# Eight conditioning slices in seven places, ahead of the second half of w_in

## What is computed

```python
cs = silu(c)                                  # 9 conditioning rows of 1024
mod = cs @ w_ada + b_ada                      # w_ada is 1024 x 6144, in float32 24 MB
sh1, sc1, g1, sh2, sc2, g2 = split(mod, 6)
h = rmsnorm(x, norm1_g) * (1 + sc1) + sh1
proj = h @ w_in                               # then two mixers (gated linear attention, windowed attention)
bias = rel_bias[rel_bucket(distance)]         # a table by distance, used by the attention later
```

## Time and profile before

| | |
|---|---|
| median of 3 runs | 1361.9 us (1361.71 to 1362.45) |
| the profiled execution | 1366.18 us, of which the span from first to last instruction is 1364.6 |
| busy, share of the span | TensorE 83%, DVE 51%, ACT 45%, POOL 9% |
| mean granted TensorE clock | 0.918 of full speed |
| moved by DMA | 234.43 MB, mean 172 GB/s |

### The profile page before, as it was taken

One profiled execution on the slowest core, in us unless ns is written; L12 is line 12 of the kernel. 1 busy time (PEld: TensorE's weight loads), 2 busy tenths in 40 slices (PEclk: granted clock), 3 DMA queues, 4 the chain that ended last, 5 costly groups with the idle time before them and its releaser, 6 DMA issues.

```text
span 1364.6 us, 18815 instructions
## 1 busy us (share of the span) xinstructions
PE 1126.3 (83%) x6935; PEld 630.3 (46%) x6936; DVE 702.5 (51%) x1099; ACT 607.8 (45%) x939; POOL 118.8 (9%) x135
## 2 busy tenths in 40 slices
PE   3799999898989898996799980089999999999800
PEld 0255656465656566664445540034444444444400
DVE  2356545454444444346333336257558658655557
ACT  2256553444454545345311121157557557555434
POOL 0000000000000000000100003320112111111032
PEclk9799988899999999998889995589999999999955
DMA  9664410605050413822325310569868798768255
GB/s 356 245 215 149 129 49 10 185 1 155 1 147 10 119 37 96 306 94 64 99 73 170 131 66 7 202 215 381 327 246 307 271 344 322 267 247 332 108 200 188
DMA packets 122341, 234.43 MB, mean 172 GB/s; under 512 B 11079, under 2 KB 54569, under 8 KB 119200
## 3 DMA queue, kind: packets, MB, share of 16 engines
q1 hardware_dynamic: 111760, 200.37, 43.1%
q0 software_dynamic: 7200, 21.06, 4.3%
q10 hardware_dynamic: 3312, 12.06, 2.2%
HBM read 197.60 MB, written 35.64 MB: 171 GB/s over the span
## 4 chain that ended last, share of the span: by engine, by line
PE 65%; DVE 12%; DMA 10%; issue 5%; ACT 5%; POOL 2%; SPq 0%; POOLq 0%; ACTq 0%; DVEq 0%
PE banks L1605 7%; PE banks L1606 7%; PE banks L1607 7%; PE banks L1971 4%; PE banks L1972 4%; PE banks L1973 4%; DMA arena<-in_moe_w_gate_dram 3%; PE banks L1793 3%; PE banks L1821 3%; PE banks L1807 3%; DVE arena L1496 2%; DVE arena L1264 2%; PE banks L1912 2%; DMA arena<-in_w_ada_dram 2%; PE banks L1913 2%
## 5 line engine op out<-in xcount | busy, mean ns | idle before, releaser
L1496 DVE SCALAR_TENSOR_TENSOR arena<-arena 128x2048 f16<-128x2048 f32 x96 | 217.5, 2288 | 82.7 <-ACT arena L972 82.7
L972 ACT ACTIVATE arena<-arena 128x2048 f16<-128x2048 f32 x96 | 180.2, 1906 | 94.2 <-DMA arena<-in_moe_w_up_dram 57.9
L1605 PE MATMUL banks<-arena 128*128 128x384 f16 (+5 forms) x576 | 193.4, 336 | 11.9 <-DVE arena L1158 8.2
L1606 PE MATMUL banks<-arena 128*128 128x384 f16 (+5 forms) x576 | 192.8, 335 | 0.0
L1607 PE MATMUL banks<-arena 128*128 128x384 f16 (+5 forms) x576 | 192.5, 334 | 0.0
L1971 PE MATMUL banks<-arena 128*128 128x512 f16 x368 | 141.5, 385 | 10.5 <-DVE arena L1509 10.4
L1972 PE MATMUL banks<-arena 128*128 128x512 f16 x368 | 141.2, 384 | 0.0
L1973 PE MATMUL banks<-arena 128*128 128x512 f16 x368 | 141.0, 383 | 0.0
L867 ACT ACTIVATE arena<-banks 128x512 f32<-128x512 f32 (+3 forms) x96 | 49.3, 513 | 128.7 <-PE banks L1807 128.7
L1264 DVE CUSTOM_DVE_ANT_0 arena<-banks,arena 128x128 f32<-128x128 f32 (+7 forms) x96 | 72.3, 754 | 45.9 <-PE banks L1793 45.7
L859 ACT ACTIVATE arena<-arena 128x128 f32<-128x128 f32 (+7 forms) x96 | 74.3, 774 | 28.8 <-DVE arena L1267 27.5
(11 more groups left out here) (308 smaller groups left out, 1704.3 us busy)
## 6 DMA issues: line engine op xcount, KB each, us to landing
arena<-in_moe_w_gate_dram SPq DMA_DIRECT2D x32, 1024.0 KB, 8.4
arena<-in_moe_w_up_dram SPq DMA_DIRECT2D x32, 1024.0 KB, 8.3
arena<-in_moe_w_down_dram SPq DMA_DIRECT2D x32, 1024.0 KB, 6.3
arena<-in_w_ada_dram SPq DMA_DIRECT2D x24, 1024.0 KB, 5.3
slot_rows<-arena ACTq DMA_DIRECT2D x23, 512.0 KB, 6.4
out_dram<-arena SPq DMA_DIRECT2D x20, 512.0 KB, 3.1
arena<-in_w_in_dram SPq DMA_DIRECT2D x18, 512.0 KB, 6.6
arena<-in_x_prompt_dram SPq DMA_DIRECT2D x16, 512.0 KB, 8.2
```

The source lines that it names most:

```text
L972: A(w_hi[s][p // 2][:, (p % 2) * PIECE:(p % 2 + 1) * PIECE], stage[g % RING], ACT.Copy, scale=WS).then_inc(phi_ok, 1)
L1496: v.scalar_tensor_tensor(out=w_lo[s][p // 2][:, part], in0=stage[(PIECES * s + p) % RING], scalar=WS, in1=w_hi[s][p // 2][:, part], op0=AL ...
L1605: mm(out, hTh[:, k, tok], wh(k), start=(first and k == ks[0]), stop=False)
L1606: mm(out, hTh[:, k, tok], wl(k), start=False, stop=False)
```

## The change

- Slices 0 to 7 get seven places: the three of before and four more in the region of hTh and hTl. Slice 7 goes to place 0 again, when slice 0's products are done; from there on the slices take the first three places in turn.
- On SP half 1 of w_in and tile 1 of x are moved from before slice 0 to behind slice 7; tile 0 of x is moved behind slice 2.
- On TensorE the bias table's products are moved from behind slice 3 to ahead of slice 0.
- On ACT the high split of half 1 and the `rms` of tile 1 are moved: the split behind the copy of the shift rows, `rms(1)` behind `high_hT(0)`.
- On DVE the low split of half 0 is moved behind the copies of the bias table, the low split of half 1 behind `low_hT(0)`, `norm(1)` behind that.
- `eps` and `one` stand behind the identity in the list of constants and are loaded with it (130 columns in place of 128). `rms(0)` waits for that load alone. All constants after the identity up to `tokid` stand two columns (8 bytes) later.

```diff
-for _name, _w in (("ident", P), ("ones", P), ("cum_mid", P), ...
+for _name, _w in (("ident", P), ("eps", 1), ("one", 1), ("ones", P), ("cum_mid", P), ...
...
-        wa = [V(o_r + s * 2 * D, 2 * D) for s in range(SLICES)]
+        wa = [V(o_r + s * 2 * D, 2 * D) for s in range(SLICES)] + [V(A_HT + s * 2 * D, 2 * D) for s in range(EARLY)]
+
+        def slice_place(n):
+            return n if n < SLICES + EARLY else (n - SLICES - EARLY) % SLICES
...
-            sp.dma_start(ident, consts[:, 0:P]).then_inc(id_in, 16)
+            sp.dma_start(V(A_CONST, P + 2), consts[:, 0:P + 2]).then_inc(id_in, 16)
...
             def load_slice(n):
-                if n >= SLICES:
-                    sp.wait_ge(ada_ps, 4 * (n - SLICES + 1))
-                sp.dma_start(wa[n % SLICES], ...
+                if n >= SLICES + EARLY:
+                    sp.wait_ge(ada_ps, 4 * (n - SLICES + 1 if n >= 2 * SLICES + EARLY else n - SLICES - EARLY + 1))
+                sp.dma_start(wa[slice_place(n)], ...
...
-            for j in range(2):
+            def load_wG(j):
                 k = slice(4 * j, 4 * j + 4)
                 sp.dma_start(wG[:, k], w_in_v[:, k, 0:GW]).then_inc(wG_in[j], 16)
-                load_x(j)
+            load_wG(0)
             for n in range(3):
                 load_slice(n)
+            load_x(0)
             load_ba(0)
             sp.dma_start(gbc, norm1_g[0:1, :].partition_broadcast(P)).then_inc(ba_in, 16)
             for n in range(3, 8):
                 load_slice(n)
-            sp.dma_start(V(A_CONST + P, oh_at - P), consts[:, P:oh_at]).then_inc(const_in, 16)
+            load_wG(1)
+            load_x(1)
+            sp.dma_start(V(A_CONST + P + 2, oh_at - P - 2), consts[:, P + 2:oh_at]).then_inc(const_in, 16)
...
                 if t == 0:
-                    act.wait_ge(const_in, 32)
+                    act.wait_ge(id_in, 16)
...
             rms(0)
-            rms(1)
             act.wait_ge(row_ps, 2)
             A(bcS1, banks[:, 0:D], ACT.Copy).then_inc(bc_ok, 1)
+            split_wG_high(1)
             high_hT(0)
+            rms(1)
...
             bo.done(v.tensor_copy(sbias, banks[0:NB * HD, 1536:1536 + CK + 1]), wait=False)
+            split_wG_low(0)
             add_bias(0)
...
             norm(0)
+            low_hT(0)
+            split_wG_low(1)
             norm(1)
-            low_hT(0)
...
-            for n in range(4):
-                ada_slice(n)
             pe.wait_ge(bias_ps, 1)
...
             mm(banks[0:NB * HD, 1536:1536 + CK + 1], relr, ohs, start=True, stop=True).then_inc(bias_ps, 1)
-            for n in range(4, KC):
+            for n in range(KC):
                 ada_slice(n)
```

More of the change, by code:

```diff
@@ L55 @@
 RING = 4
-SLICES = 3
+SLICES, EARLY = 3, 4
 EPS = 1e-6
@@ L78 @@
 _at = 0
-for _name, _w in (("ident", P), ("ones", P), ("cum_mid", P), ("cum", P), ("cum_rest", P), ("strict", P),
+for _name, _w in (("ident", P), ("eps", 1), ("one", 1), ("ones", P), ("cum_mid", P), ("cum", P), ("cum_rest", P), ("strict", P),
                   ("blk", HA * DV), ("oh", GN), ("ohs", CK + 1), ("seq8", NB), ("diag8", NB * HD),
                   ("eprio", NE), ("gprio", NG), ("thr", NT), ("before", NE * NE), ("srows", 1), ("tokid", NT),
-                  ("eps", 1), ("one", 1), ("head12", HD), ("quad", 4)):
+                  ("head12", HD), ("quad", 4)):
     _cols[_name] = (_at, _w)
@@ L360, in build @@
         cleared = sem("cleared"); silu_c = sem("silu_c"); csT_ps = sem("csT_ps")
-        csT_ok = sem("csT_ok"); ada_in = [sem(f"ada_in{s}") for s in range(SLICES)]; ba_in = sem("ba_in"); mod_in = sem("mod_in"); row_ps = sem("row_ps"); id_in = sem("id_in"); oh_in = sem("oh_in"); ada_ps = sem("ada_ps")
+        csT_ok = sem("csT_ok"); ada_in = [sem(f"ada_in{s}") for s in range(SLICES + EARLY)]; ba_in = sem("ba_in"); mod_in = sem("mod_in"); row_ps = sem("row_ps"); id_in = sem("id_in"); oh_in = sem("oh_in"); ada_ps = sem("ada_ps")
         ada_added = sem("ada_added"); bc_ok = sem("bc_ok")
@@ L425, in load_slice @@
             def load_slice(n):
-                if n >= SLICES:
-                    sp.wait_ge(ada_ps, 4 * (n - SLICES + 1))
-                sp.dma_start(wa[n % SLICES], w_ada_v[:, n % KC, bass.ds(n // KC * 2 * D, 2 * D)]).then_inc(ada_in[n % SLICES], 16)
+                if n >= SLICES + EARLY:
+                    sp.wait_ge(ada_ps, 4 * (n - SLICES + 1 if n >= 2 * SLICES + EARLY else n - SLICES - EARLY + 1))
+                sp.dma_start(wa[slice_place(n)], w_ada_v[:, n % KC, bass.ds(n // KC * 2 * D, 2 * D)]).then_inc(ada_in[slice_place(n)], 16)
             def load_ba(q):
@@ L732, in _, with split_wG_high @@
             A(csT[:, :, 0:NB + 1], bank(7, KC * (NB + 1)).rearrange("p (k m) -> p k m", k=KC), ACT.Copy).then_inc(csT_ok, 1)
-            for j in range(2):
+            def split_wG_high(j):
                 act.wait_ge(wG_in[j], 16)
@@ L736, in _ @@
                 A(wGh[:, k], wG[:, k], ACT.Copy, scale=WS).then_inc(whi_ok, 1)
+            split_wG_high(0)
             def rms(t):
@@ L1067, in _, with split_wG_low @@
                           relx.rearrange("p (c h) -> p c h", c=PAIRS).unsqueeze(2).broadcast_to([33, PAIRS, NB, 2])).then_inc(bias_ps, 1)
-            for j in range(2):
+            def split_wG_low(j):
                 k = slice(4 * j, 4 * j + 4)
@@ L1582, in ada_slice @@
             def ada_slice(n):
-                pe.wait_ge(ada_in[n % SLICES], 16 * (n // SLICES + 1))
+                early = SLICES + EARLY
+                pe.wait_ge(ada_in[slice_place(n)], 16 if n < early else 16 * ((n - early) // SLICES + 2))
                 if n == 2 * KC:
@@ L1587, in ada_slice @@
                 for j in range(4):
-                    mm(bank(4 if q == 0 else 2)[32 * j:32 * j + 32], csT[:, k], wa[n % SLICES][:, 512 * j:512 * j + 512],
+                    mm(bank(4 if q == 0 else 2)[32 * j:32 * j + 32], csT[:, k], wa[slice_place(n)][:, 512 * j:512 * j + 512],
                        start=(k == 0), stop=(k == KC - 1)).then_inc(ada_ps, 1)
```

## The result

In the first comparison the changed kernel took 1352.34 us (median of 20 runs) beside 1361.44 of the kernel before (20 runs): a ratio of 0.9939, 95% interval 0.9917 to 0.9961, or 9.1 us (5.3 to 11.3). A second one, made with the last experiments, gave 1351.62 (6 runs) beside 1364.1 (11 runs): 0.9908, interval 0.9882 to 0.9934, or 12.5 us (9.0 to 16.1). The forecast was 1353.0, 8.9 us less.

What follows compares the result with a forecast made beforehand. A chain of waits, mostly transfers up to 43 us, was taken as the bound; 8.9 us less (some 5.1 bytes moved back, 3.8 the hole) took the median from 1361.9 to 1353.0 us, range 1349.5 to 1357.5.

Steps and rivals of the forecast that it cites:

- The arrival of the eighth slice: At the start, by bytes in one ordered queue: slice 7 used at 34.0 us, not 42.91, a gain of 8.9.
- the rival of a queue without order: Slice 7 shares the DMA engines with loads behind it: used near 40.7, gain 2.2, 1359.7 us; chance 0.05.
- Bytes moved back: 2.13 MB needed later (half of w_in, tile 1 of x) leaves the queue ahead of slice 7: some 5.1 us.
- The hole: DMA stops from 36 to 37 us as slice 7's load waits for slice 4's products behind the bias products: 3.8 us.
- 5.0 us of cover: Bias products ahead of slice 0 on TensorE cost nothing; were their cover gone, 5.0 us.
- The high split of half 1: On ACT, behind the shift rows' copy: ends 3.2 us before the copy of the turned tile is wanted, so hidden.
- norm 1: On DVE, the norm of tile 1 ends 0.5 us before TensorE wants it, after slice 8's products.
- x 2 hang on the same events as before: On the SP queue, the load of x's tile 2 was taken to be triggered as before, with no cost given.
- The constants' wait: Tile 0's root no longer waits for the constants; that wait ended before the rows were spread, so no gain.
- The faster clock: Rival: TensorE at the higher clock shortens slice 7 (0.9) and the spread rows (1.0): 1351.1 us; chance 0.17.
- The staging place: Expert weights' fourth place, shifted 8 bytes: taken as 0, up to +7 us; chances 0.06 part of bound, 0.04 slower experts.
- The whole: The 8.9 us gained early lasts to the end, as TensorE hardly rests from 61.9 us on: 1353.0 us.

Runs made afterwards that it cites:

- after: The first profiled execution of the changed kernel, no further edit; it took 1349.44 us.
- e4: The changed kernel again, no edit, for a second trace; 1348.17 us.
- e5: The changed kernel with small constants reordered so that the fourth staging place of the expert weights is no longer 8 bytes off; 1360.46 us, one run.
- e6: The changed kernel with the other three staging places of the expert weights moved by 56 bytes, so all four are off a 64-byte boundary; 1349.59 us, one run.
- e11: The changed kernel, no edit, timed again in the last comparison; 1351.62 us, ratio 0.9908 to the kernel before.
- e2: The changed kernel with half 1 of w_in and tile 1 of x back ahead of the slices; 1359.65 us, ratio 0.9979 to the kernel before.
- e1: The kernel before with only the bias table's products moved ahead of slice 0, loads and three places unchanged; 1359.99 us, ratio 0.9979.
- e3: The changed kernel with the bias table's products back between slices 3 and 4; 1353.89 us, one run.
- e7: The changed kernel with half 0 of w_in and its splits moved too, so both halves load behind slice 7; 1353.73 us, ratio 0.9931 to before.
- e8: The kernel before again, no edit, for a second trace; 1361.01 us.
- e9: The changed kernel with both halves of w_in behind slice 7 and, on ACT, tile 1's copy ahead of x 2's statistics; 1351.69 us, ratio 0.9912 to before.

## Why the prediction was right

**The arrival of the eighth slice.** Forecast: used at 34.0 us, 23.9 behind half 0. Measured: 34.97, 33.81, 35.24, 34.46 and 34.68 in the five traces with the changed order (after, e4, e5, e6, e11), a mean of 24.17 behind half 0. Counting bytes in one queue served in order was right within 0.3 us from half 0, 0.6 from the span's start, and the rival of a queue without order (40.7) is excluded.

**The two terms.** Bytes moved back: 5.1 forecast, 5.3 measured by e2 and 6.4 by e1. The hole: 3.8 forecast, 3.7 by e2 against the traces of before, 2.2 to 2.9 by e1. Their sum of 8.9 became 9.0 at slice 7. At the first projection it is 9.2: a mean of 56.6 in the two traces of before, 47.4 in the five.

**What filled the hole.** The prediction gave the bias products 5.0 us of cover and told nothing of which part removes the hole. e1 and e3 showed that either does: with the new order of the bytes the seven places do it without the move of the bias products (e3), and with the old order and three places that move does it (e1).

**What was moved behind it.** The high split of half 1 was to be hidden by 3.2 us and was by 2.3; norm 1 by 0.5 and was by 1.2. Both held. The 3.2 was a slip: the copy of the shift rows, which the split follows, begins at A + 5.0 and ends at A + 6.0, so the prediction's own rows give 2.2. One step was wrong in its reason: "x 2 hang on the same events as before". Its issue does, but it lands behind what is still queued, 8.7 us after its issue instead of 4.5. It cost TensorE nothing in the five traces of the changed order, though in three of them the copy of tile 1 began late by it, and 0.50 us in e7. The step looked at when a load is asked for, not at what stands ahead of it then.

**The constants' wait.** "It gains nothing" held where the spread rows took 2.09 us; in e8 the wait cost 0.6. The change makes that case impossible, so in these traces this is at most 0.6 us of the gain.

**The faster clock.** The rival came true in part, but differently in each execution, and in the kernel before as well (e8: slice 7 in 1.07 us, the spread rows in 1.75), so these traces do not show it to be an effect of the change: slice 7 took 1.76 us in the first trace, 1.94 in e4, 1.07 in e5, and the spread rows 1.14 in e6 beside 2.09 in most. It was priced at 1.9 us for these two; on the path it gave 0 to 1.3. The Trainium skill (TensorE: Matmul & The Clock Gate, HAM oscillation) has the rate fall over idle gaps between bursts. e3 agrees, where slices without a gap took 1.39; closer slices alone, 0.55 us apart, did not keep the rate in the first trace, where slices 4 and 5 took 1.94 and 1.93, and in e8 slice 7 had the higher one after an idle time of 2.96 us.

**The staging place** was priced at 0 with +7 kept (seven pieces at 1.1 us would be 7.7), and e5 and e6 show no cost.

**The whole.** That a us gained ahead of the first projection is a us gained at the end was taken from TensorE's full stretch behind it. The medians agree, 9.1 and 12.5 with intervals that share 9.0 to 11.3. That the first median lies within 0.7 us of the forecast is in part luck, with an interval of 3 us to either side. Whether the change adds up to 2 us more behind the first projection stays open.

## What to carry to other kernels

Find what the first full stretch of the busiest engine waits for, count the bytes ahead of it in its queue, and move back what is needed later; that count gave the arrival here to 0.3 us. More buffers and an earlier place for the work that blocks them fill the same hole, so price them together and not one by one. Then read which load is now last in the fuller queue and what stands behind its consumer on that engine: here loading the other half of w_in behind the slices too gained 2 to 3 us at the first projection, uncovered one Square ahead of a copy, which took 0.5 back; no median showed the gain.

## What the hardware showed that was not expected

- **An issue takes time when the queue is full.** SP spent 5.24 us on the issue of x 1 and 3.88 on the first part of the constants, beside 0.79 and 0.43 in the kernel before. In e7, x 1 took 8.67. In e2 the constants were issued in 0.43 with some 6.6 MB ahead of them, in the changed kernel in 3.88 with some 7.1 (bytes issued less bytes moved, an estimate); what it is that fills is not shown. The engine that issues is held, with everything behind it.
- **The clock column can hide the lower level.** In e4 it reads 0.50 at a slice of 1.93 us (23.8 to 25.8) and 1.00 at one of 1.07 (31.3 to 32.4). In the first trace it reads 1.00 from 0 to 30 us, while the slices take 1.93 to 1.94 there. The durations decide.
- **The start itself varies.** The same first load was ready at 9.99 to 11.72 us in executions that have the same loads ahead of it, and all behind it moved along.
- **The rest of the kernel varies by several us.** Behind the first projection, the five traces of the changed order took 1299 to 1311 us, and e9, with the same work there, 1296.5. One pair of traces cannot give the worth of a change of this size; only the stretch that the change touches can.
